# A hybrid decoder layer on one core: the transposes of one block of attention probabilities moved from TensorE to VectorE

## The reference

```
h = rms_norm(x);  z = h @ w_in -> q, k, v (3 groups x 8 heads x 64), u, gate_a, gate_s
a = dilated_attention(q, k, v)        # groups with dilation 1, 4, 16; softmax statistics shared
s = GLU(gelu(S5 state space model(u)))
x = x + (sigmoid(gate_a) * (a @ w_attn_proj) + sigmoid(gate_s) * s) @ w_out
x = x + (silu(h2 @ w_gate) * (h2 @ w_up)) @ w_down,   h2 = rms_norm(x)
```

## Time and profile before

| what | value |
|---|---|
| median of 3 runs | 872.07 us (870.81 to 874.33) |
| the profiled execution | 871.46 us |
| its span | 869.7 us |
| mean granted TensorE clock | 0.998 |
| DVE busy in the span | 66% |
| ACT busy in the span | 42% |

### The profile page before, as it was taken

One profiled execution on the slowest core, in us unless ns is written; L12 is line 12 of the kernel. 1 busy time (PEld: TensorE's weight loads), 2 busy tenths in 40 slices (PEclk: granted clock), 3 DMA queues, 4 the chain that ended last, 5 costly groups with the idle time before them and its releaser, 6 DMA issues.

```text
span 869.7 us, 15093 instructions
## 1 busy us (share of the span) xinstructions
PE 857.5 (99%) x5203; PEld 733.8 (84%) x5203; DVE 571.6 (66%) x749; ACT 366.3 (42%) x575; POOL 271.8 (31%) x275
## 2 busy tenths in 40 slices
PE   9999999999999999999999999999999999999998
PEld 7788788888887878878887888779999999888886
DVE  5558976577924444544587556989999999533334
ACT  6312343323246666746433343344555445222221
POOL 3789995010020000001220221455666664000000
PEclk9999999999999999999999999999999999999999
DMA  8439237634365452413544233223343333222222
GB/s 307 145 104 235 75 122 148 219 132 142 109 217 166 152 155 82 143 50 99 153 139 187 80 98 95 86 84 98 101 116 113 105 97 119 75 96 96 96 72 98
DMA packets 103495, 108.89 MB, mean 125 GB/s; under 512 B 11712, under 2 KB 69296, under 8 KB 103328
## 3 DMA queue, kind: packets, MB, share of 16 engines
q1 hardware_dynamic: 96544, 94.25, 34.5%
q10 hardware_dynamic: 5504, 10.52, 3.8%
q0 software_dynamic: 1408, 3.61, 2.0%
HBM read 94.38 MB, written 13.96 MB: 125 GB/s over the span
## 4 chain that ended last, share of the span: by engine, by line
PE 48%; DVE 5%; POOL 1%; issue 1%; ACT 0%; DMA 0%; SPq 0%; ACTq 0%; POOLq 0%
PE ps L1842 18%; PE ps L1862 13%; PE ps L1529 12%; PE ps L1804 4%; DVE w_lo L672 1%; DVE late L1403 1%; DVE late L1511 1%; DVE w_lo L1415 0%; DVE h_lo L1411 0%; ACT w_hi L666 0%; DVE late L1378 0%; DVE late L1339 0%; DMA w_raw<-in_w_ffn_up 0%; DVE hT_lo L1345 0%; POOL late L643 0%
## 5 line engine op out<-in xcount | busy, mean ns | idle before, releaser
L672 DVE TENSOR_TENSOR w_lo<-w_raw,w_hi 128x1024 fp32r<-128x1024 f32 x109 | 143.6, 1318 | 207.8 <-ACT w_hi L666 207.6
L666 ACT ACTIVATE w_hi<-w_raw 128x1024 fp32r<-128x1024 f32 x109 | 115.3, 1058 | 279.5 <-PE ps L1529 157.5
L1529 PE MATMUL ps<-w_hi,hT_hi 128*128 128x512 f32 x280 | 109.8, 392 | 1.8 <-DVE w_lo L672 1.1
L1529 PE MATMUL ps<-w_lo,hT_hi 128*128 128x512 f32 x280 | 109.0, 389 | 0.0
L1529 PE MATMUL ps<-w_hi,hT_lo 128*128 128x512 f32 x280 | 109.0, 389 | 0.0
L496 POOL TENSOR_TENSOR early<-early 128x16 f32<-128x16 f32 (+6 forms) x129 | 91.4, 708 | 23.0 <-ACT early L689 13.1
L1529 PE MATMUL ps<-hT_hi,w_hi 128*128 128x512 f32 x224 | 91.5, 409 | 0.0
L1529 PE MATMUL ps<-hT_hi,w_lo 128*128 128x512 f32 x224 | 87.7, 392 | 0.0
L1529 PE MATMUL ps<-hT_lo,w_hi 128*128 128x512 f32 x224 | 87.4, 390 | 0.0
L1842 PE MATMUL ps<-h_hi,w_hi 128*128 128x256 f32 x256 | 73.2, 286 | 2.7 <-DVE late L1378 2.7
L1842 PE MATMUL ps<-h_lo,w_hi 128*128 128x256 f32 x256 | 73.2, 286 | 0.0
(11 more groups left out here) (247 smaller groups left out, 1809.1 us busy)
## 6 DMA issues: line engine op xcount, KB each, us to landing
w_raw<-in_w_in SPq DMA_DIRECT2D x108, 256.0 KB, 3.4
w_raw<-in_w_ffn_down SPq DMA_DIRECT2D x44, 256.0 KB, 2.8
w_raw<-in_w_ffn_gate SPq DMA_DIRECT2D x64, 128.0 KB, 2.2
w_raw<-in_w_ffn_up SPq DMA_DIRECT2D x64, 128.0 KB, 2.3
z_d<-early ACTq DMA_DIRECT2D x7, 1024.0 KB, 4.9
late<-z_d SPq DMA_DIRECT2D x96, 64.0 KB
w_raw<-in_w_out SPq DMA_DIRECT2D x16, 256.0 KB, 2.8
late<-z_d SPq DMA_DIRECT2D x12, 256.0 KB
```

The costliest lines, as they stand in the source:

```text
L666: nc.scalar.activation(w_hi[:, j % WSPL], w_raw[:, j % WRAW], ACT.Copy).then_inc(w_hi_done, 1)
L672: nc.vector.tensor_tensor(w_lo[:, j % WSPL], w_raw[:, j % WRAW], w_hi[:, j % WSPL].bitcast(F32), ALU.subtract).then_inc(w_lo_done, 1)
L1529: ins = T.matmul(ps[:, bank0 + m], lhsT, rhs, start=first and h == 0 and k == 0, stop=last and h == 1 and k == 2)
```

## The change

The last 128 columns of each probability block no longer go through PE. DVE turns them with its transpose of 32x32 blocks, from `prob` straight into `probT`; since everything outside the diagonal 32x32 blocks is zero, this is the same matrix. `turn_prob` on PE does one transpose less, ACT's copy out of bank 6 ends at column 384 and no longer at 512. `prob` has four buffers, in separate places, so that the exponentials of step u wait for the turns of step u - 4, on PE and on DVE. DVE's `turn_class` is called behind the maxima of u = 3, 5 and 7 for the two steps (u - 3, u - 2), and at u = 8 for steps 6 and 7. Each waits for the exponentials of its step and, from step 4 on, for the value products that read that `probT` buffer. `values` on PE waits in addition for both of its class turns. DVE's weight remainder of u = 7 moves to u = 8, behind the last turns.

```diff
-        prob = off(8704, 1024).rearrange("p (b k) -> p b k", b=2)
+        prob = [off(a, 512) for a in (8704, 9216, 13856, 14368)]
...
+        class_turned = sem("class_turned")
...
-                            if u >= 2:
-                                act.wait_ge(prob_turned, 8 * i + u - 1)
+                            if u >= 4:
+                                wait_apart(act, (prob_turned, 8 * i + u - 3), (class_turned, 8 * i + u - 3))
...
-                            nc.scalar.activation(probT[:, v % 4, k0:512], ps[:, 6, k0:512], ACT.Copy).then_inc(misc_act, 1)
+                            nc.scalar.activation(probT[:, v % 4, k0:384], ps[:, 6, k0:384], ACT.Copy).then_inc(misc_act, 1)
...
+            def turn_class(i, v):
+
+                dve.wait_ge(prob_done, 8 * i + v + 1)
+                if v >= 4:
+                    dve.wait_ge(o_done, 4 * i + v // 2 - 1)
+                V.transpose(probT[:, v % 4, 384:512], prob[v % 4][:, 384:512]).then_inc(class_turned, 1)
...
+                        if u in (3, 5, 7, 8):
+                            for v in ((u - 3, u - 2) if u % 2 else (6, 7)):
+                                turn_class(i, v)
...
-                        if u in (1, 4, 7):
-                            lo(W_GATE + u // 3 + 2 + 4 * i, u // 3 + 2)
+                        if u in (1, 4, 8):
+                            lo(W_GATE + (u + 1) // 3 + 2 - u // 8 + 4 * i, (u + 1) // 3 + 2 - u // 8)
...
-                for x in range(0 if u // 2 else 1, 4):
-                    ins = T.transpose(ps[:, 6, x * P:(x + 1) * P], prob[:, u % 2, x * P:(x + 1) * P], ident[:, :])
+                for x in range(0 if u // 2 else 1, 3):
+                    ins = T.transpose(ps[:, 6, x * P:(x + 1) * P], prob[u % 4][:, x * P:(x + 1) * P], ident[:, :])
...
                 pe.wait_ge(misc_act, MA_Y + ma_probT(2 * n + 1) + MA_PAIR * i)
+                pe.wait_ge(class_turned, 8 * i + 2 * n + 2)
```

More of the change, by code:

```diff
@@ L809, in _ @@
                             n, h = u // 2, u % 2
-                            if u >= 2:
-                                act.wait_ge(prob_turned, 8 * i + u - 1)
+                            if u >= 4:
+                                wait_apart(act, (prob_turned, 8 * i + u - 3), (class_turned, 8 * i + u - 3))
                             k0 = 0 if n else P
-                            nc.scalar.activation(prob[:, u % 2, k0:256], negs[:, u % 2, k0:256], ACT.Exp, scale=-1.0,
+                            nc.scalar.activation(prob[u % 4][:, k0:256], negs[:, u % 2, k0:256], ACT.Exp, scale=-1.0,
                                                  bias=ost[b][:, 0, n, h, 0:1],
                                                  accum_out=ost[b][:, 0, n, h, 1:2])
-                            nc.scalar.activation(prob[:, u % 2, 256:512], negs[:, u % 2, 256:512], ACT.Exp, scale=-1.0,
+                            nc.scalar.activation(prob[u % 4][:, 256:512], negs[:, u % 2, 256:512], ACT.Exp, scale=-1.0,
                                                  bias=ost[b][:, 1, n, h, 0:1],
```

## The result

The changed kernel takes 878.66 us in the median of 6 runs (877.49 to 881.43), the kernel before in its 6 runs beside it 871.33: a ratio of 1.0091 with a 95% interval of 1.008 to 1.0101, slower by 7.3 us. The profiled execution took 878.77 us, with a span of 877.0. Forecast were 878.7, in a range of 874.5 to 884.0; that was 6.6 us more than the 872.07 of the kernel before that the prediction started from.

A forecast was written before the change was run, and what follows sets the result against it. PE sets the pace, a pair every 37.9 us. Pauses at values(1) +3.9 net of saved turns, stage end +0.5, clock +2.2, on 871.46: 878.1, as a median 878.7 us; range 874.5 to 884.

The forecast's parts named there:

- The wait of values(1): At u = 5 PE pauses 2.5 us for turns 2 and 3, behind the u = 4 remainder and maxima(5) on DVE.
- The transposes: On DVE, two 128x128 transposes in a row take 0.50 us, bounds 0.26 and 2.2; spaced in full by the skill, 0.62.
- The balance of a pair: Per pair 1.99 later at values(1), -0.78 scores(3) wait, -0.33 shorter turns, +0.10 waits: +0.98 us; four pairs +3.9.
- The end of the stage: Turns 6 and 7 delay the last remainder and gate_out; DVE's part moves 1.46, PE's 0.98: +0.5 us once.
- The clock: Behind one or two of the four pauses the granted clock falls, 1.5 us each: +2.2 us, bounds 0 and 6.
- The four buffers: Four probability buffers relax a wait of ACT's exp that stands behind its wait for the maxima; relief costed at nothing.
- The lateness between pairs: Between pairs the lateness meets a slack of some tenths; costed at nothing, up to 0.5 us a pair without that cover.
- values(0), (2) and (3): Turns for values(0) and (2) are hidden; for values(3), 0.50 us fits before the moved remainder, if barely.
- The gain on PE: Rival: turns 2 and 3 done in time, PE keeps 0.88 us a pair less 0.2: 2.7 us, 869.4; 7%.

The follow-up runs named there:

- the fastest version: The changed kernel with DVE's weight remainder of u = 4 moved behind maxima(5) and turns 2 and 3; 865.66 us, ratio 0.9947 to the kernel before.
- the kernel with doubled turns: The changed kernel with turns 2 and 3 each made twice on DVE, first into memory nothing reads; 881.66 us, ratio 1.0117 to the kernel before.

## Why the prediction was right

- **The wait of values(1).** Foreseen was a pause of 2.5 us, a start at 315.2 on the old scale, released by DVE's turn. Measured: 2.36 us, four times, released by L1235, and a start 18.02 us behind the pair's first scores (299.51 to 317.53), which is 315.09 on the old scale. Moving the turns or the remainder removes the pause, which shows the cause.
- **The transposes.** Taken were 0.50 us for two, from the copy of the same size. The row of the changed kernel has exactly 0.50, with a median of 0.278 us for one (0.262 to 0.311). The Trainium skill ("VectorE: DVE Perf Modes", section "The three transpose paths") has 311 ns for bf16; the float32 ones here were a little shorter, and two overlapped, so the estimate of 0.62 us from that page was too high. Two figures beside it were loose: 0.12 us more for two turns is 0.5 to 0.6 over the four pairs and not 0.7, and the lower bound of 0.26 us for two has no working; two copies of 174 ns are 0.35 in full.
- **The balance of a pair.** Foreseen +0.98 us without the clock, measured +1.1 (39.04 against 37.93 in the third pair). The sum is close because errors in its terms offset one another: 0.22 too much up to values(3), 0.35 too little behind it. Up to values(1) the third pair is 1.88 us longer, not 1.99; up to values(3) it is 0.76 longer, where the sum had 0.98. The added waits of PE, which I took at 0.05 each, don't show: in the two kernels with the remainder behind maxima(5), the one with the turns on DVE reaches values(3) 0.88 us earlier in the pair (25.59 against 26.47 us), all that eight turns are worth. Then 0.35 us is lost again between values(3) and the next pair, the wait of L1764 for L1227 shown above. I had named that lateness and put it at nothing; it was there, inside the 0.5 that I gave as its bound.
- **The end of the stage.** The sum took another 0.5 us, since DVE would be later than PE at the second weight behind the stage. Those products of PE began 5.73 us behind the first ones (409.86 to 415.59) where they took 5.61 (401.25 to 406.86): 0.1, or 0.2 by the weight loads in front of them (409.82 to 415.59, 401.24 to 406.77), an oversized term. DVE's gate_out was later than PE by 0.3 and not by 0.5 (409.03 against 400.12, PE 409.86 against 401.25).
- **The clock.** I took one or two falls at 1.5 us each. The profiled run had three in the stage, and a pair with a fall was 1.57 us longer than one without. The fall at 588 us was missing, which I had not thought of, so the net was two. Over the single runs the time follows the mean clock: 877.49 us at 0.996, 878.46 to 878.95 at 0.994, 881.43 at 0.990. The profiled runs with one fall have a mean clock of 0.997 or 0.998, the one with three 0.994 and the one with four 0.992; by that, four of the change's six runs had about three falls (an estimate), and most runs of the kernel before one.
- **How much was luck.** That the forecast of 878.7 and the median of 878.66 all but agree is luck. The increase was 7.3 us and not 6.6; the kernel before came out 0.7 us faster beside the change (871.33) than the prediction started from (872.07). Within the 7.3, the pause and what hangs on it came to 4.2 (forecast 4.4) and the clock to 3.1 (forecast 2.2). What was not luck is the place of the wait, what releases it, its length, and that the clock would fall behind some of the pauses.
- **Costed at nothing.** The four buffers: right, as far as 0.998 to 1.001 can tell (870.53 against 871.32). The lateness between pairs: wrong by 0.35 us a pair, see above. values(0), (2) and (3): right, no wait for a transpose but the four was recorded. For values(3) this goes with the remainder moved to u = 8: with it back at u = 7, tried in the fastest version only, PE waits there.
- **The gain on PE.** Foreseen 0.88 us a pair less 0.2 for waits, 2.7 in all; measured, in the two kernels with the remainder of u = 4 behind maxima(5), 2.5. The make-up is another: 4 x 0.88, less three times the 0.35 between pairs.

## What to carry to other kernels

Work moved from the engine that sets the pace to an idle one gains only if the new producer's place in its own in-order queue is ahead of the moment at which the consumer comes. So find the instruction in front of it that itself waits longest, here a remainder waiting for ACT, and put the new work ahead of that or that behind the new work. A pause of PE can have a second price, the clock of what follows. It is not charged each time: of pauses of the same length in one execution some had a fall of the clock behind them and one had not. And look at what the new work makes late behind it in its own queue, not only at who waits for it: here DVE's later `gate_out` and copies cost another 0.35 us a pair, at a place where no transpose is waited for.

## What was not expected of the hardware

The granted clock did not follow from the length of a pause alone. It fell behind three of four pauses of 2.36 us in one execution and behind all four of 2.7 us in another, but not behind the one of 2.49 us at 597 us in the changed kernel, nor at the same place behind 2.47 us in the kernel with doubled turns. In the other eight profiled runs, where that pause took 2.46 to 2.73 us, there was a fall. It did not fall behind the four pauses of 1.2 us. Each fall lasted about 3.4 us at 1.2 GHz. One cost 1.57 us in a pair of the change, 1.5 behind 588 us (there worked out from the matmuls' spacing). What else decides was not tried and stays open.
